# Stages of a two-layer encoder ordered by token tiles: values first in the mixer, dense gates and ups by tokens, normalisation tile by tile

## The reference

```python
z = x @ w_in                         # pool part, q and k, v, output gate, 8 gate columns
y = concat(pool_mixer(z_pool), mlstm(silu(conv(z_qk)), z_v, gates) * sigmoid(z_o))
h = layer_norm(ALPHA * x + y @ w_out)
f = swiglu(h, wg, wu, wd)            # layer 0: dense, 2816 hidden channels
f = sum over the top 2 of 8 experts of weight * swiglu(h, ...)   # layer 1: 3584 hidden channels each
x = layer_norm(ALPHA * h + f)
```

## Time and profile before

| | us |
|---|---|
| median of three runs (lowest, highest) | 1372.56 (1372.14, 1373.38) |
| the profiled execution | 1376.61 |
| its span, first to last instruction | 1374.8 |
| TensorE busy in it | 1306.0 |
| span up to the first expert product | 456.17 |

### The profile page before, as it was taken

How to read it: one execution, slowest core, us unless ns; L and a number is a source line. 1 busy time by engine, 2 the same in 40 slices (tenths; PEclk the granted TensorE clock), 3 DMA queues, 4 the chain that set the end, 5 groups by cost and what they waited for, 6 DMA issues and landing times.

```text
span 1374.8 us, 18075 instructions
## 1 busy us (share of the span) xinstructions
PE 1306.0 (95%) x6708; PEld 1089.8 (79%) x6708; DVE 1118.6 (81%) x936; ACT 929.3 (68%) x733; POOL 126.7 (9%) x127
## 2 busy tenths in 40 slices
PE   7998999998998899999999999999999999999995
PEld 7897999987897777777876777877777787777773
DVE  5867544456867789999798999879899979899996
ACT  6543444445444488788787888778788878788882
POOL 3445000003553000000000000000000000000001
PEclk9999999998997799999999999999999999999999
DMA  9535655551524789999999999999999999999992
GB/s 328 195 99 202 211 190 188 188 186 62 184 93 153 279 311 389 372 406 398 399 409 383 369 393 396 408 376 410 349 371 410 395 405 409 403 366 394 398 405 88
DMA packets 132913, 425.25 MB, mean 309 GB/s; under 512 B 8992, under 2 KB 11328, under 8 KB 132816
## 3 DMA queue, kind: packets, MB, share of 16 engines
q1 hardware_dynamic: 131168, 419.16, 80.8%
q0 software_dynamic: 1504, 4.76, 1.1%
q10 hardware_dynamic: 144, 0.07, 0.0%
HBM read 422.91 MB, written 1.05 MB: 308 GB/s over the span
## 4 chain that ended last, share of the span: by engine, by line
PE 76%; DVE 14%; issue 6%; ACT 3%; SPq 1%; DMA 1%; DVEq 0%; ACTq 0%
PE bank L1671 19%; PE bank L1672 18%; PE bank L1673 18%; DVE w_lo L1125 8%; PE bank L1971 6%; PE bank L1972 6%; PE bank L1945 2%; DVE w_lo L1139 2%; DVE arena L1211 1%; PE bank L2017 1%; PE bank L1967 1%; PE bank L1968 1%; PE bank L2004 1%; DMA raw<-in_w_in 1%; ACT w_hi L789 1%
## 5 line engine op out<-in xcount | busy, mean ns | idle before, releaser
L1125 DVE TENSOR_TENSOR w_lo<-raw,w_hi 128x2048 fp32r<-128x2048 f32 x216 | 486.1, 2283 | 50.0 <-PE bank L1673 23.9
L789 ACT CAST w_hi<-raw 128x2048 fp32r<-128x2048 f32 x216 | 407.1, 1913 | 76.1 <-PE bank L1673 74.4
L1671 PE MATMUL bank<-w_hi,parts 128*128 128x512 f32 x824 | 330.1, 401 | 14.4 <-DVE w_lo L1125 7.7
L1673 PE MATMUL bank<-w_hi,parts 128*128 128x512 f32 x824 | 323.1, 392 | 0.0
L1672 PE MATMUL bank<-w_lo,parts 128*128 128x512 f32 x824 | 323.1, 392 | 0.0
L1971 PE MATMUL bank<-w_hi,parts 128*128 128x512 f32 x672 | 272.0, 405 | 8.9 <-ACT arena L991 3.1
L1972 PE MATMUL bank<-w_lo,parts 128*128 128x512 f32 x672 | 264.2, 393 | 0.0
L1139 DVE TENSOR_TENSOR w_lo<-raw,w_hi 128x2048 fp32r<-128x2048 f32 x61 | 141.4, 2320 | 99.0 <-PE bank L1673 97.5
L1671 PEld LDWEIGHTS bank<-w_hi,parts 128*128 128x128 f32 x824 | 155.9, 189 | 56.8 <-issue 13.3
L804 ACT CAST w_hi<-raw 128x2048 fp32r<-128x2048 f32 x61 | 116.3, 1910 | 117.3 <-PE bank L1673 111.8
L1125 DVE TENSOR_TENSOR w_lo<-arena,w_hi 128x2048 fp32r<-128x2048 f32 x80 | 181.3, 2283 | 13.7 <-ACT w_hi L789 6.2
(11 more groups left out here) (238 smaller groups left out, 1134.7 us busy)
## 6 DMA issues: line engine op xcount, KB each, us to landing
raw<-in_wu_exp SPq DMA_DIRECT2D x76, 1024.0 KB, 9.6
raw<-in_wg_exp SPq DMA_DIRECT2D x70, 1024.0 KB, 8.3
raw<-in_wd_exp SPq DMA_DIRECT2D x70, 1024.0 KB, 10.4
arena<-in_wd_exp SPq DMA_DIRECT2D x29, 1024.0 KB, 10.6
arena<-in_wg_exp SPq DMA_DIRECT2D x26, 1024.0 KB, 10.8
arena<-in_wu_exp SPq DMA_DIRECT2D x25, 1024.0 KB, 9.2
raw<-in_w_in SPq DMA_DIRECT2D x20, 1024.0 KB, 6.7
tokens<-in_wg_exp SPq DMA_DIRECT2D x16, 1024.0 KB, 11.1
```

The costliest lines, as they stand in the source:

```text
L789: a.copy(to, ring[s]).then_inc(hi_ready, 1)
L1125: v.tensor_tensor(low(n), ring[s], high(n).bitcast(F32), ALU.subtract).then_inc(lo_ready, 1)
L1671: mm(psum, left[0], right[0], start=first, stop=False)
L1673: return mm(psum, left[1], right[0], start=False, stop=last)
```

## The change

The mixer's kinds go in the order v, q, k, p, o, w. v is made tile by tile (`values(t)`), and the gate columns follow it in both layers. A norm's tile 0 is transposed on PE among the last products of tile 1 (`turn(2 * l + 1, 0)` inside `project`, `turn(2, 0)` inside `down`), and tile 1 after the first product of the next stage for tile 0 (`turn(1, 1)`, `turn(2 * l, 1)`). ACT and DVE finish each tile's scaling and splitting before the other's, with `ahead` in between. The projection runs units 1 to 3 for tile 0, then for tile 1. In the dense stage gates and ups are made by tokens, in four banks; silu and the multiplication work on 128 x 512, and the product is transposed on PE (`hidden_turn`) before it is split. POOL's convolutions are 2 and 3, and silu 3 comes last. The first router logits stand inside the projection. Two `ahead` of DVE and one of ACT around the routing move, and the last two of the five small products get a bank and a signal of their own. At the start SP loads tile 0 of x, unit 0, tile 1, unit 1, and then the gate columns.

```diff
-MIXER_KINDS = [(k, h) for k in "qkvpo" for h in range(2)] + ...
+MIXER_KINDS = [(k, h) for k in "vqkpo" for h in range(2)] + ...
-        POOL_CONVS = (3, 6)
+        POOL_CONVS = (2, 3)
+        SILU_ORDER = (0, 1, 2, 4, 5, 6, 7, 3)
...
@@ sync @@
-            for t in range(TT):
-                sp.dma_start(tokens[:, t, :], x_d[:, t, :]).then_inc(x_in[t], 16)
-            for l in range(LAYERS):
-                sp.dma_start(gate_raw[:, l, :, :], ...)
             for n, (kind, half) in enumerate(MIXER_KINDS):
+                if n < TT:
+                    sp.dma_start(tokens[:, n, :], x_d[:, n, :]).then_inc(x_in[n], 16)
                 load(mixer_unit(0, kind, half), mixer_source(0, kind, half))
+                if n == TT - 1:
+                    for l in range(LAYERS):
+                        sp.dma_start(gate_raw[:, l, :, :], ...)
...
@@ scalar, mixer @@
+                ahead()
                 copies("q", 0)
-                ahead()
                 silu(0)
                 silu(1)
                 ahead()
                 silu(2)
-                silu(3)
+                ahead()
                 copies("k", 4)
-                ahead()
                 silu(4)
...
                 silu(7)
-                ahead()
+                silu(3)
...
+            def norm(s):
+                norm_std(s, 0)
+                ahead()
+                tile(s, 0)
+                if s == 3:
+                    token_high(0)
+                norm_std(s, 1)
+                tile(s, 1)
+                ahead()
...
@@ vector, mixer @@
                 ahead()
+                for t in range(TT):
+                    dve.wait_ge(*chunk_event(l, "v", t))
+                    ...
+                    v.tensor_copy(v_sb[:, t, :], bank[t][:, :]).then_inc(v_ready, 1)
+                    ahead()
...
                 conv(1)
                 ahead()
-                conv(2)
                 ahead()
                 conv(4)
                 conv(5)
                 ahead()
+                conv(6)
                 conv(7)
-                ahead()
-                for t in range(TT):
-                    dve.wait_ge(*chunk_event(l, "v", t))
...
@@ vector, norm @@
                 for t in range(TT):
                     for n in range(2):
                         residual_half(s, t, n)
                     normalise(s, t)
-                turn(s)
+                    if s < 3 or t == 0:
+                        ahead()
+                    tile(s, t)
+                    if s < 3:
+                        x_low(s, t)
...
@@ tensor, mixer @@
+                def values(t):
+                    for half in range(2):
+                        n = mixer_unit(l, "v", half)
+                        if t == 0:
+                            arrived(n)
+                        tile_arrived(2 * l, t, half)
+                        ...
+                        if l and (t, half) == (0, 0):
+                            turn(2 * l, 1)
+                for t in range(TT):
+                    values(t)
+                gates()
...
+                chunks("q", 0, lambda c: (v_ready, TT * l + min(c + 1, TT)))
+                chunks("q", 1)
...
@@ tensor, projection @@
+                        if (t, q, half) == (1, 2, 0):
+                            turn(2 * l + 1, 0)
+                        elif l and (t, q, half) == (1, 3, 0):
+                            logits(0, range(DK))
...
@@ tensor, dense @@
+                def gate_up(kind, b, half, t):
+                    ...
+                    for kk, k in enumerate(ks):
+                        last = product(psum, x_parts(k, slice(t * P, (t + 1) * P)), (hi[:, kk, :], lo[:, kk, :]),
+                                       k == 0, k == DK - 1)
+                def hidden_turn(b):
+                    for t in range(TT):
+                        pe.wait_ge(dh_ready, TT * b + t + 1)
+                        for j in range(dense_chunks(b)):
+                            last = tr(dense_turn_bank(b, t)[:, j * P:(j + 1) * P], dsg[:, t, j * P:(j + 1) * P], ident)
+                        last.then_inc(dturn, 1)
```

More of the change, by code:

```diff
@@ L941, in dense, with silu @@
-                for kind, b, half in DENSE_ORDER[:-1]:
-                    ahead()
-                    if kind == "u" and half == (1 if b < DENSE_BLOCKS - 1 else 0):
-                        c0, n = 4 * b, dense_chunks(b)
-                        silu(c0)
-                        for c in range(c0 + 1, c0 + n):
-                            silu(c)
-                            hidden_hi(c - 1)
-                        hidden_hi(c0 + n - 1)
-            turn(0)
-            for _ in range(HI_AHEAD):
-                ahead()
+                def silu(b, t):
+                    act.wait_ge(*dense_event("g", b, t))
+                    if b:
+                        act.wait_ge(dturn, TT * b)
+                    w = dense_chunks(b) * P
+                    a.activation(dsg[:, t, 0:w], bank[GATE_BANKS[t]][:, 0:w], ACT.Silu).then_inc(dsilu, 1)
@@ new lines, in hidden_hi @@
+                def hidden_hi(b, t):
+                    n = dense_chunks(b)
+                    act.wait_ge(dturn, TT * b + t + 1)
+                    if b >= 2:
+                        act.wait_ge(unit_done, dense_unit("d", b - 2, 1) + 1)
+                    a.copy(dh_hi[:, b % 2, 0:n, t * P:(t + 1) * P],
+                           dense_turn_bank(b, t)[:, 0:n * P].rearrange("p (j c) -> p j c", c=P)).then_inc(dhi_ready, 1)
+                for unit in DENSE_ORDER[:-2]:
+                    kind, b, half = unit
+                    ahead()
+                    for c in range(DENSE_BLOCKS):
+                        if unit == dense_turned_after(c):
+                            for t in range(TT):
+                                hidden_hi(c, t)
+                    if kind == "g" and half == dense_halves(b) - 1:
+                        for t in range(TT):
+                            silu(b, t)
@@ new lines, in tile @@
+            def tile(s, t):
+                dve.wait_ge(turned, 2 * (TT * s + t) + 2)
+                if s == 1 and t == 0:
+                    dve.wait_ge(par_ready, 2)
+                for k in range(DK // 2, DK):
+                    src = bank[TURN_BANKS[t][1]][:, (k - 4) * P:(k - 3) * P]
+                    if s == 0:
+                        v.tensor_copy(xf[:, t, k, :], src).then_inc(xf_dve, 1)
+                    else:
+                        norm, l = NORM[s]
+                        v.tensor_scalar(xf[:, t, k, :], src, par_col((norm, "g"), l, k),
+                                        par_col((norm, "b"), l, k), ALU.mult, ALU.add).then_inc(xf_dve, 1)
@@ L1226, in mixer @@
                 ahead()
+                conv(6)
                 conv(7)
-                ahead()
-                for t in range(TT):
-                    dve.wait_ge(*chunk_event(l, "v", t))
-                    if l and t == 0:
-                        dve.wait_ge(tokens_ready, TT * 2)
-                    v.tensor_copy(v_sb[:, t, :], bank[4 + t][:, :]).then_inc(v_ready, 1)
                 dve.wait_ge(cols_mm, l + 1)
@@ L1381, in norm @@
                     normalise(s, t)
-                turn(s)
-            turn(0)
-            for _ in range(AHEAD):
+                    if s < 3 or t == 0:
+                        ahead()
+                    tile(s, t)
+                    if s < 3:
+                        x_low(s, t)
+            for t in range(TT):
+                tile(0, t)
+                x_low(0, t)
                 ahead()
```

425 lines of the change are left out of this document (190 added, 235 removed).

## The result

The changed kernel takes 1360.71 us (median of 4 runs, 1358.93 to 1364.50) against 1372.70 us (4 runs, 1372.14 to 1373.38). The ratio is 0.990, 95% interval 0.988 to 0.992: 11 to 16 us less. On another chip, beside the kernels of the last experiments, it was 0.991 (0.990 to 0.993). The forecast was 1357.5 us in a range of 1348 to 1369. The profiled execution took 1359.08 us, its span is 1357.3.

A forecast was written before the change was run, and what follows sets the result against it. PE's program order bounds the first 456 us, by its waits and the 1.2 GHz clock behind them. Terms -5.4 - 10.4 + 1.5 - 0.8 = -15.1 us: 1361.5 from the profiled 1376.61, 1357.5 as median; range 1348 to 1369.

The forecast's parts named there:

- The forecast's own signs: Checks named beforehand: PE waits at the norm, layer 1's scores, wait ahead of scores, dense stage length, first expert product.
- The v copies and the gate chain in layer 1, -10.4: Layer 1 up to its scores: v first and gates beside q remove waits of 3.3 and 1.3 us; 10.4 us less.
- the 60.3 of the working: Predicted length in us of layer 1 up to the scores, against 70.7 before: 53.2 + 1.4 + 2.4 + 0.8 + 2.5.
- The wait of 2.4 us ahead of the scores with a fall of the clock behind: Both mixers: PE waits for DVE from 53.1 to 55.5 us after v starts; 2.5 us charged for the clock.
- the 31.0 of the working: Layer 0: predicted start of the q products in us, after v ends at 26.8 and gate columns add 3.6.
- Norm 1, -5.4: Norm 1 with the dense stage: two PE waits of 0.7 us, clock held, against 6.7 lost before; 5.4 us less.
- its split ends near T + 8.2: Norm 1: tile 0's split is done 8.2 us after its projection ends (T), before PE needs it at T + 9.2.
- Tile 1 is ready at T + 12.6, PE at T + 11.9: 0.7: Norm 1, counted from the end of tile 0's projection (T): PE waits only 0.7 us for normalised tile 1.
- The dense stage, net 0: Gates and ups by tokens save 5.8 us, 44 added transposes of hidden values cost 5.7; net 0.1, nothing.
- The rival by which they break the stream: Dense stage: hidden transposes make PE wait or drop the clock, 5.1 us six times; 1388 us, chance 0.07.
- Projections and routing, 0 and -0.8: Scores to the dense stage: no change; layer 1's scores to the first expert product: 0.8 us less, bounds -4 and +2.
- All of it arrives: Experts: an earlier first expert product moves the stream of loads by as much, so the whole gain reaches the end.

The follow-up runs named there:

- e4: Kernel before the change, with only the v copies moved from DVE to ACT, between silu 5 and silu 6: 1364.13 us, 0.993 of before.
- c0_changed: The changed kernel itself, run again on another chip beside three of its variants: 1362.19 us, 0.991 of before.
- e1: Changed kernel with POOL's row products at norms 1 and 2 waiting for DVE's low half of that tile: 1359.95 us, 0.990 of before.
- e2: Changed kernel with the projection's last weight unit rounded and subtracted ahead of the low half of y's last part: 1364.06 us, 0.994 of before.
- e6: Changed kernel with the expert unit behind norm 3 moved up behind tile 0's copies, on DVE and ACT: 1363.58 us, 0.990 of before.
- e8: Changed kernel with three edits: POOL's rows behind the low halves, last weight unit sooner, norm 3's expert unit moved up: 1357.63 us, 0.987 of before.
- c8: The three-edit kernel of e8 run again, beside the changed kernel on one chip: 1356.79 us against 1362.19, 0.989 of before.
- c7: Changed kernel with 20 one-column copies added on ACT in the dense stage, beside the changed kernel: 1365.07 us against 1362.19, 0.994 of before.
- e3: Changed kernel with its three norms undone, both tiles transposed behind the whole projection or last down product: 1363.09 us, 0.993 of before.

## Why the prediction was right, and where it was wrong

Faster came in, by waits that left the mixers, and the time lies in the range. The forecast's own signs mostly did not. The scores of layer 1 stand 59.6 us behind norm 2, as said. But PE waits 3.4 us ahead of the second tile's transposes (L1692, now L1713) and not under 1, the dense stage takes 193.9 us and not 189 to 192, the wait of 2 to 3 us ahead of the scores is 0.7 in layer 0 and missing in layer 1, and the first expert product at 446.19 lies just on the wrong side of "after 446 us". So the number is in part luck: errors of several us stand against each other. By its steps:

*The v copies and the gate chain in layer 1, -10.4.* The two waits left as forecast, and the stretch gave -11.1. e4 shows by itself that the v copies' wait, with some of the low clock behind it, is worth 4 to 5 of this. But the 60.3 of the working hold 3.3 us (0.8 and 2.5) that lie behind the scores. Up to the scores it has 57.0, and 59.6 were measured: 3.5 for 1.4 at the norm, and two falls of the clock, against no wait at the scores. That the two figures agree is luck.

*The wait of 2.4 us ahead of the scores with a fall of the clock behind.* It was 0.72 and nothing. DVE was ready when forecast, 38.2 us behind the gate columns in layer 1 (38.4 in the working), and POOL's meeting with two weight units came too:

```profile
348.47 4.96 POOL L742 TENSOR_SCALAR arena<-arena,par 128x256 f32<-128x256 f32 x1
```

But PE was not there by 36.0: it took 38.4, in part at a clock of 0.92 (the window from 360 us on above), with no wait ahead of the fall (it began at 358.4 us and lasted 3.4). In layer 0 the q products began 0.6 us sooner than the 31.0 of the working, DVE was ready 0.8 sooner, and neither the 0.8 behind the scores nor the fall that I had taken 1.5 for came: those four make the 3.8 us by which layer 0 beat its term. In c0_changed the clock did fall there, and the scores still came at 68.98, 0.5 later.

*Norm 1, -5.4.* Wrong: -1.8. The step that failed is "its split ends near T + 8.2" and, from it, "Tile 1 is ready at T + 12.6, PE at T + 11.9: 0.7". The split met POOL's product and took 4.08 us for 1.4; DVE came to the sums of tile 1 2.7 us later than in e1 (119.23 for 116.48); the wait was 3.4 us and not 0.7, and the clock, taken as held, fell at both norms. The prediction had the lock in its list, with its size from the earlier trace rows, and looked for it at convolution 2 alone. POOL's row products start at the moment in which a tile is normalised, which is now the middle of DVE's fullest stretch.

*The dense stage, net 0.* Nearly. From one hidden transpose to the next it takes 33.54 us per block, where the down products of before stood 33.94 apart (206.07 and 240.01):

```profile
208.52 1.03 PE L1905 MATMUL bank<-cst,arena 128*128 128x128 f32 x8
...
242.06 1.04 PE L1905 MATMUL bank<-cst,arena 128*128 128x128 f32 x8
```

So 0.4 is won per block, some 2 us in all if every block gives it; the transposes cost 0.8 of the 1.04, since their tail lies under the next product (it starts at 209.31). The rival by which they break the stream is out: there is no wait ahead of any. No run undoes the dense gates by tokens alone; a version with 256 columns was not measured, so this rests on the rows.

*Projections and routing, 0 and -0.8.* Wrong by 2.6 and 3.4 (in the first 0.8 is only moved: the transposes of tile 0 now stand there). The last weight unit behind the low half of y made PE wait 1.5 us in each layer, which the working passed over (e2 removes it). In layer 1 the logits are used 60.6 us behind the scores for 56.6, 4.0 later where 2 was forecast. POOL's rows of tile 1 held DVE's comparison for 1.7 us, which the working passed over too (e6 removes it). The removed weight unit gave back what was forecast, 2.2 for 2.3: the first expert product waits 1.19 for 3.39 us. The profile names no releaser, but in both kernels the product starts 0.1 us behind the end of DVE's second low part, and in before a weight unit stands ahead of that part:

```profile
452.58 0.68 DVE L1631 CAST parts<-bank 128x512 fp32r<-128x512 f32 x1
453.18 2.28 DVE L1125 TENSOR_TENSOR w_lo<-raw,w_hi 128x2048 fp32r<-128x2048 f32 x1
455.38 0.68 DVE L1631 CAST parts<-bank 128x512 fp32r<-128x512 f32 x1
```

```profile
444.80 1.28 DVE L1653 CAST parts<-bank 128x512 fp32r<-128x512 f32 x2
```

With e2's and e6's edits in (e8, c8) the stretch from the scores to the first expert product is 71.8 us, 1.0 under before, which is the -0.8 of the forecast.

*All of it arrives.* Taken at 1:1, and it cannot be read from one execution. By the medians the gain is 12.0 us, by the marks ahead of the experts 10.0, and c7 puts some 3 us of the gain on ACT's wait. The rest moves by several us in either direction with the clock. The same stretch of the first pair, from 20 us behind the first expert product on, in before and after:

```profile
476.17:486.17 10.00, 10.00 (x55) 8.68 (x54) 3.96 (x3) 4.47 (x4) 0.00 (x0) 0.83 0.68 245
```

```profile
466.19:476.19 10.00, 10.00 (x62) 8.84 (x62) 5.35 (x7) 5.12 (x5) 0.00 (x0) 1.00 0.69 253
```

PE is busy all the time in both; in one the clock is 0.83, in the other 1.00, and seven products more are done. e1 and e4 fell there as before did, e2 and e3 did not. Nor is it the start alone. In c0_changed the same kernel came to its first expert product at the same 446.19 us, and its clock fell 64 us behind it, where that of the first profile did not; its rest is 5 us longer. What decides stays open.

So errors partly cancelled: norm, projections and routing gave 9.6 us less than forecast, the two mixers up to their scores 4.5 more, and the experts, taken at nothing, 2 by the medians and 7.5 in the one profile.

## What to carry to other kernels

- Where POOL starts a product over SBUF by an event, look at what DVE does from that event on, at every such place: each two-input operation, and each scaling within SBUF, can wait for all of POOL's. Operations of DVE with an input from PSUM can be put there in their place.
- A wait of PE in the middle of a mixer can be worth more than its length (in layer 0 the scores came 4.4 us sooner without a wait of 3.3); ask first whether another engine can do the one copy that it waits for, before the order of the products is changed.
- Compare a kernel by a mark at the end of what was changed as well as by its whole time, and count each engine's instructions ahead of a loop: 20 small copies on an engine with time to spare cost 2.9 us, 600 us further on. A stop without a releaser at a loop's jump back is the sign to look for.

## What the runs showed of the hardware

- The lock between POOL and DVE takes, besides subtractions with two SBUF inputs, DVE's scaling of 128 x 1024 from SBUF to SBUF (0.81 us alone, 2.11 beside POOL) and comparisons of 128 x 64 (1.90 for 0.21), and lengthens POOL's too (4.3 to 5.6 us for 2.4). Sums with one input in PSUM (0.68) and statistics (0.69) are not held.
- ACT can stand still for 5.1 to 5.3 us at a loop's jump back with nothing to wait for: at the same jump in all four profiles with 376 or 380 instructions ahead of the loop, with packets of its instruction queue landing meanwhile, and in none of the ten with 356.
- The granted clock fell to its lower level in a stretch in which PE never idled in some executions, and did not in others with the same instructions. From the first expert product to DVE's first table copy it takes 119.6 to 119.8 us in the four profiles without a fall, 121.6 to 122.0 in the five with one, and 121.9 to 122.6 in the five with two.
